# A residual that is transposed while its last projection still runs, into operand buffers of its own

## The reference

```python
x = x + merged @ w_out[l]                                    # block 1: "wo1";  block 2: "wo2"
h2 = rmsnorm(x, norm2_g[l])                                  # gain norm2_g;    block 2: g_mlp
x = x + jnp.square(jax.nn.relu(h2 @ w_mlp_in[l])) @ w_mlp_out[l]   # 2048 -> 8192 -> 2048: "h1","o1"; "h2","o2"
```

## Time and profile before

| | |
|---|---|
| median of 3 runs | 2964.06 us (2962.98 to 2964.64) |
| the profiled execution: time | 2963.64 us |
| the profiled execution: span, first to last instruction | 2961.7 us |
| PE busy | 2918.7 us, 99% of the span |
| PE weight loads | 2403.7 us, 81% |
| DVE, ACT busy | 1730.3 us (58%), 1367.7 us (46%) |
| mean granted clock of PE | 0.996 |
| DMA | 561 MB, mean 189 GB/s |

### The profile page before, as it was taken

One profiled execution on the slowest core, in us unless ns is written; L12 is line 12 of the kernel. 1 busy time (PEld: TensorE's weight loads), 2 busy tenths in 40 slices (PEclk: granted clock), 3 DMA queues, 4 the chain that ended last, 5 costly groups with the idle time before them and its releaser, 6 DMA issues.

```text
span 2961.7 us, 33940 instructions
## 1 busy us (share of the span) xinstructions
PE 2918.7 (99%) x13892; PEld 2403.7 (81%) x13892; DVE 1730.3 (58%) x1835; ACT 1367.7 (46%) x1570; POOL 60.3 (2%) x34
## 2 busy tenths in 40 slices
PE   8999999999999999999999999999999999999998
PEld 6788878888878888888888787888887888888886
DVE  6588854456655455554556678866655555455554
ACT  5544444554445444444445444444445444444443
POOL 1100000011000000000000000000000000000000
PEclk9999999999999999999999999999999999999999
DMA  8566755555655656555556656666555555656554
GB/s 281 165 195 196 203 167 184 179 160 188 209 174 185 198 174 203 185 181 188 195 179 228 182 170 192 198 192 210 179 201 180 190 185 183 197 175 203 186 179 155
DMA packets 290746, 561.01 MB, mean 189 GB/s; under 512 B 17696, under 2 KB 24608, under 8 KB 289952
## 3 DMA queue, kind: packets, MB, share of 16 engines
q1 hardware_dynamic: 290592, 558.85, 58.9%
HBM read 556.68 MB, written 2.10 MB: 189 GB/s over the span
## 4 chain that ended last, share of the span: by engine, by line
PE 77%; issue 18%; DVE 3%; POOL 1%; ACT 1%; DMA 0%; DVEq 0%; SPq 0%; ACTq 0%; POOLq 0%
PE ACC L569 75%; PE TB L525 2%; DVE WL L1232 1%; DVE CA L1667 1%; POOL QKV L1810 0%; ACT WH L820 0%; DMA RAW<-in_w_in_dram 0%; DVE X L1630 0%; DVE WGC L1715 0%; DVE X L1588 0%; PE TB L771 0%; ACT JK L838 0%; DMA SS<-in_x_t_dram 0%; POOL SS L1797 0%; POOL SS L1794 0%
## 5 line engine op out<-in xcount | busy, mean ns | idle before, releaser
L1232 DVE TENSOR_TENSOR WL<-RAW,WH 128x1024 fp32r<-128x1024 f32 (+1 forms) x1024 | 1252.7, 1239 | 883.1 <-ACT WH L820 881.5
L820 ACT ACTIVATE WH<-RAW 128x1024 fp32r<-128x1024 f32 (+1 forms) x1024 | 1063.3, 1054 | 973.3 <-PE ACC L569 913.5
L569 PE MATMUL ACC<-WH,XTH 128*128 128x512 f32 (+1 forms) x2720 | 1071.9, 394 | 30.3 <-DVE WL L1232 24.8
L569 PE MATMUL ACC<-WH,XTL 128*128 128x512 f32 (+1 forms) x2720 | 1060.1, 390 | 0.0
L569 PE MATMUL ACC<-WL,XTH 128*128 128x512 f32 (+1 forms) x2720 | 1058.7, 389 | 0.0
L569 PEld LDWEIGHTS ACC<-WH,XTH 128*128 128x128 f32 x2720 | 513.1, 189 | 139.5 <-DVE WL L1232 19.7
L569 PEld LDWEIGHTS ACC<-WH,XTL 128*128 128x128 f32 x2720 | 512.7, 189 | 107.4
L569 PEld LDWEIGHTS ACC<-WL,XTH 128*128 128x128 f32 x2720 | 513.5, 189 | 102.4
L569 PE MATMUL ACC<-WH,YAH 128*128 128x512 f32 x864 | 338.6, 392 | 0.0
L569 PE MATMUL ACC<-WH,YAL 128*128 128x512 f32 x864 | 336.5, 389 | 0.0
L569 PE MATMUL ACC<-WL,YAH 128*128 128x512 f32 x864 | 336.1, 389 | 0.0
(11 more groups left out here) (247 smaller groups left out, 1066.9 us busy)
## 6 DMA issues: line engine op xcount, KB each, us to landing
RAW<-in_w_in_dram SPq DMA_DIRECT2D x256, 512.0 KB, 4.3
RAW<-in_w_mlp_in_dram SPq DMA_DIRECT2D x128, 512.0 KB, 3.9
RAW<-in_w_mlp_out_dram SPq DMA_DIRECT2D x128, 512.0 KB, 4.5
RAW<-in_w_up_dram SPq DMA_DIRECT2D x128, 512.0 KB, 3.9
RAW<-in_w_down_dram SPq DMA_DIRECT2D x128, 512.0 KB, 4.6
RAW<-in_w_gate_dram SPq DMA_DIRECT2D x96, 512.0 KB, 4.0
RAW<-in_w_branch_dram SPq DMA_DIRECT2D x48, 512.0 KB, 4.4
RAW<-in_w_out_dram SPq DMA_DIRECT2D x32, 512.0 KB, 4.6
```

Source lines behind the costliest of these rows:

```text
L569: ins = e.matmul(ACC[:, 2 * (b % 2) + half, 0:n], p[:, k, xs], q[:, t, 0:n], start=(k == 0 and m == 0), stop=(k == nk - 1 and m == 2))
L820: e.activation(WH[u % NSPL][:, :, 0:n], RAW[u % NRAW][:, :, 0:n], ACT.Copy).then_inc(hi, 1)
L1232: e.tensor_tensor(l, r, h, ALU.subtract).then_inc(lo, 1)
```

## The change

Two buffer pairs are added, XBH1/XBL1 and XBH2/XBL2, [128, 16, 256] each. `turn` "x1" and "x3" write them, and all blocks of `h1` and `h2` multiply with them (`operands`). Laid out behind HB, they begin at bytes 165408 and 181792 (XBH1, XBL1) and 173600 and 189984 (XBH2, XBL2). The steps of "x1" and "x3" now stand behind units `last(w, c) + 2` and `+ 3` for each of the four blocks c, in the order that "x2" has: six of eight steps lie within `wo`, the last two behind the second and third unit of `h(0,0)`. `root` stays behind the last unit. In place of the wait for the last unit of `wo`, the first step waits for `mgv`, long past by then; "x2" waits for the last unit of `wo1`, also long past.

```diff
+    XB["1"] = sb("XBH1", [P, 16, L], F32R, m1), sb("XBL1", [P, 16, L], F32R, m1)
...
+    XB["2"] = sb("XBH2", [P, 16, L], F32R, m2), sb("XBL2", [P, 16, L], F32R, m2)
...
     for tag, w in (("x1", "wo1"), ("x3", "wo2")):
-        for _ in range(4):
-            at(("turn", tag), last(w, 3))
+        for c in range(4):
+            at(("turn", tag), last(w, c) + 2, 2)
         at(("root", tag), last(w, 3))
-        at(("turn", tag), last(w, 3) + 1, 4)
...
-            return XTH, XTL
+            return XB[kind[1]] if kind in ("h1", "h2") else (XTH, XTL)
...
-        def turn(task, done, gain):
+        def turn(task, ready, gain, to=XTH):
             for n in range(8):
                 if n == 0:
-                    multiplied(e, *done)
+                    ready()
...
-                        ins = e.activation(XTH[:, 2 * n + m, :], t[:, m * L:m * L + L], ACT.Copy, scale=gain[:, 2 * n + m:2 * n + m + 1])
+                        ins = e.activation(to[:, 2 * n + m, :], t[:, m * L:m * L + L], ACT.Copy, scale=gain[:, 2 * n + m:2 * n + m + 1])
...
-                 ("turn", "x1"): lambda: turn("x1", ("wo1", 3), VEC[:, V_N2:V_N2 + 16]),
-                 ("turn", "x2"): lambda: turn("x2", ("h1", 7, 1), gain_x2),
+                 ("turn", "x1"): lambda: turn("x1", lambda: e.wait_ge(mgv, 4), VEC[:, V_N2:V_N2 + 16], XB["1"][0]),
+                 ("turn", "x2"): lambda: turn("x2", lambda: multiplied(e, "wo1", 3), gain_x2),
...
-                 ("turn", "x3"): lambda: turn("x3", ("wo2", 3), VEC[:, V_MLP:V_MLP + 16]),
+                 ("turn", "x3"): lambda: turn("x3", lambda: e.wait_ge(mgv, 8), VEC[:, V_MLP:V_MLP + 16], XB["2"][0]),
```

More of the change, by code:

```diff
@@ L241, in build @@
     m1 = ExitStack()
-    YB, HB = {}, {}
+    YB, HB, XB = {}, {}, {}
     YB["1"] = sb("YBH1", [P, 8, L], F32R, m1), sb("YBL1", [P, 8, L], F32R, m1)
     HB["1"] = [sb(f"HB{i}1", [P, 2, 512], F32, m1) for i in range(2)]
+    XB["1"] = sb("XBH1", [P, 16, L], F32R, m1), sb("XBL1", [P, 16, L], F32R, m1)
     m1.close()
@@ L1034, in turn @@
                 if gain is None:
-                    e.activation(XTH[:, 2 * n:2 * n + 2, :], pair(t), ACT.Copy).then_inc(tx_hi, 1)
+                    e.activation(to[:, 2 * n:2 * n + 2, :], pair(t), ACT.Copy).then_inc(tx_hi, 1)
                 else:
                     for m in range(2):
-                        ins = e.activation(XTH[:, 2 * n + m, :], t[:, m * L:m * L + L], ACT.Copy, scale=gain[:, 2 * n + m:2 * n + m + 1])
+                        ins = e.activation(to[:, 2 * n + m, :], t[:, m * L:m * L + L], ACT.Copy, scale=gain[:, 2 * n + m:2 * n + m + 1])
                     ins.then_inc(tx_hi, 1)
@@ L1183, in _ @@
                  "gm0": lambda: gm_turn(0), "gm1": lambda: gm_turn(1), "at_t": at_turn, "yb": yb,
-                 ("turn", "m1"): lambda: turn("m1", ("gb", 3), None),
-                 ("turn", "x1"): lambda: turn("x1", ("wo1", 3), VEC[:, V_N2:V_N2 + 16]),
-                 ("turn", "x2"): lambda: turn("x2", ("h1", 7, 1), gain_x2),
-                 ("turn", "m2"): lambda: turn("m2", ("g2a", 3), None),
-                 ("turn", "x3"): lambda: turn("x3", ("wo2", 3), VEC[:, V_MLP:V_MLP + 16]),
+                 ("turn", "m1"): lambda: turn("m1", lambda: multiplied(e, "gb", 3), None),
+                 ("turn", "x1"): lambda: turn("x1", lambda: e.wait_ge(mgv, 4), VEC[:, V_N2:V_N2 + 16], XB["1"][0]),
+                 ("turn", "x2"): lambda: turn("x2", lambda: multiplied(e, "wo1", 3), gain_x2),
+                 ("turn", "m2"): lambda: turn("m2", lambda: multiplied(e, "g2a", 3), None),
+                 ("turn", "x3"): lambda: turn("x3", lambda: e.wait_ge(mgv, 8), VEC[:, V_MLP:V_MLP + 16], XB["2"][0]),
                  ("res", "wo1"): lambda: res_squares("wo1", R_1), ("res", "wo2"): lambda: res_squares("wo2", R_4),
@@ L1569, in branch_next, with turn @@
                 yield
-        def turn(task, gain):
+        def turn(task, gain, to=(XTH, XTL)):
             for n in range(8):
                 if gain is None:
-                    low_part(XTL[:, 2 * n:2 * n + 2, :], XTH[:, 2 * n:2 * n + 2, :], tx_hi, TX0[task] + n + 1, task, n)
+                    low_part(to[1][:, 2 * n:2 * n + 2, :], to[0][:, 2 * n:2 * n + 2, :], tx_hi, TX0[task] + n + 1, task, n)
                 else:
@@ L1579, in turn @@
                         k = 2 * n + m
-                        ins = e.scalar_tensor_tensor(out=XTL[:, k, :], in0=t[:, m * L:m * L + L], scalar=gain[:, k:k + 1],
-                                                     in1=XTH[:, k, :], op0=ALU.mult, op1=ALU.subtract)
+                        ins = e.scalar_tensor_tensor(out=to[1][:, k, :], in0=t[:, m * L:m * L + L], scalar=gain[:, k:k + 1],
+                                                     in1=to[0][:, k, :], op0=ALU.mult, op1=ALU.subtract)
                     freed(ins, task, n)
@@ L1739, in _ @@
                  ("branch", "b2a"): lambda: branch_next("b2a", "g2a", SG2, MG, 4),
-                 ("turn", "m1"): lambda: turn("m1", None), ("turn", "x1"): lambda: turn("x1", VEC[:, V_N2:V_N2 + 16]),
+                 ("turn", "m1"): lambda: turn("m1", None), ("turn", "x1"): lambda: turn("x1", VEC[:, V_N2:V_N2 + 16], XB["1"]),
                  ("turn", "x2"): lambda: turn("x2", gain_x2), ("turn", "m2"): lambda: turn("m2", None),
-                 ("turn", "x3"): lambda: turn("x3", VEC[:, V_MLP:V_MLP + 16]),
+                 ("turn", "x3"): lambda: turn("x3", VEC[:, V_MLP:V_MLP + 16], XB["2"]),
                  ("res", "wo1"): lambda: res_out("wo1"), ("res", "wo2"): lambda: res_out("wo2"),
```

## The result

The changed kernel takes 2976.16 us (median of 6 runs, 2974.72 to 2977.81), the kernel before 2964.35 us in the same rounds (2959.11 to 2965.51). The ratio is 1.0043, with a 95% interval of 1.003 to 1.0055: slower by 11.8 us. The forecast was 2977.2 us, range 2973 to 2982. The profiled execution took 2974.72 us, span 2972.7. Lines of `kernel.py` are one higher than before from the second added buffer on: line 569 is now 570, 1232 is 1233.

A forecast was written before the change was run, and what follows sets the result against it. PE, busy 99%, was taken as the bound, through its gaps and matmul pace. Terms -8.79 (stall and slow clock) + 1.4 (new wait) + 0.2 (places) + 20.3 (pace) = +13.1 us gave 2977.2 us, range 2973 to 2982.

The forecast's parts named there:

- The stall and its clock: From wo1 to h1 and wo2 to h2: PE's waits (5.73 us) and the slow clock behind them go, 8.79 us gained.
- the term of 3.06 us: Units behind PE's two 2.7 us gaps: matmuls at the lowered clock return to full pace, 3.06 us gained.
- The new wait: Third unit of h1 and h2: PE waits for a cut behind ACT's root and table load, 0.7 us each, 1.4 lost.
- Rival B: Crossings into h1 and h2: new wait longer or slow clock back, with XB's slow pace; 2980.4 us, chance 0.11.
- the wait of 2.23 us: A PE wait in the earlier trace followed by full-clock matmuls, cited for charging no slow clock to the new wait.
- The places: Within wo: four more places, twice, where a step interrupts PE's matmuls, 0.03 us each, 0.2 us lost.
- The pace: h1 and h2: 3072 matmuls load from XB at YB's pace instead of XT's, 6.6 ns each, 20.3 us lost.
- Rival A: h1 and h2: XB reads at XT's pace, so the pace term is 0; -7.1 us, 2957.0 us, chance 0.11.
- C: h1 and h2: XB slow only in part, about 10 us lost, 2967 us, no difference; chance 0.04.
- a multiple of 64: Loaded buffers: YB and XB begin 32 bytes past one, offered as one possible reason for the 6.6 ns slower pace.
- the upper part of the partition: Loaded buffers: YB and XB lie above byte 131200, offered as the other possible reason for the 6.6 ns slower pace.

The follow-up runs named there:

- e4: The changed kernel's buffers with the step and root order of the kernel before: 2981.64 us, 1.0058 of the kernel before.
- e9: The kernel before with 96 unused bytes ahead of ST, so YB begins at a multiple of 128: 2955.76 us, ratio 0.9973.
- e5: The changed kernel with 96 unused bytes ahead of ST, so XB and YB begin at multiples of 128: 2948.2 us, 0.9949 of the kernel before.
- e2: The kernel before with 32 unused bytes ahead of ST: 2960.66 us, ratio 0.9987.
- e3: The kernel before with XT moved by 32 bytes and all behind it by 64: 3009.35 us, ratio 1.0153.
- e8: e5 with the root of x1 and x3 four units later: 2949.01 us, 0.995 of the kernel before.
- e10: e5 with the moving operands WH and WL alone moved by 32 bytes: 3020.39 us in one execution.
- e6: e5 with all buffers from X on moved by 32 bytes, all distances kept: 2949.62 us, 0.9951 of the kernel before.
- e11: e5 with loaded pairs at chosen distances past the moving operand (YB1 128, XB1 64, YB2 32, XB2 256 bytes): 2966.3 us in one execution.
- e12: e5 with loaded pairs at chosen distances past the moving operand (YB1 384, XB1 16, YB2 96, XB2 192 bytes): 2966.62 us in one execution.
- e7: e5 with loaded pairs offset from a multiple of 128 (YB1 4, XB1 16, XB2 64, YB2 96 bytes; low parts another 128): 2966.89 us, one execution.

## Why the prediction was right

**The stall and its clock, 8.79 us.** Both waits of 2.7 us and both slow stretches are gone. Taken alone, the order gave 5.7 us (e4 against the changed kernel) and 8.3 us (e9 against e5) for a forecast of 8.79 - 1.4 - 0.2 = 7.2. Each is the difference of two ratios whose intervals are some 3 to 4.5 us to either side, so 5.7 and 8.3 can't be told apart. The traces say more. From PE's wait near 630 us to the one near 1590, and from the one near 1815 us to the end, e5 is 3.4 and 3.2 us shorter than e9, 6.6 in all; the changed kernel is 1.9 and 3.3 shorter than e4. The 1.9 belongs to the crossing of e4 at which the clock stayed full. For the slow clock after the gap is not certain: in the five kernels of this study that keep the 2.7 us wait (before, e2, e3, e4, e9) the low clock followed it in 8 of 10 places, so the term of 3.06 us is what one trace showed and not what every execution pays.

**The new wait, 0.7 us each.** It stands where the working put it, and is 0.60 and 0.61 us long; it brought no slow clock back. Rival B is out. e8 shows that it comes from the root ahead of the cut. That no slow clock followed waits this short held in all traces; the wait of 2.23 us that the prediction named beside them was luck of that trace, as the last section shows.

**The places, 0.2 us.** Steps lie within `wo1` as planned, with 19.08 us for 84 matmuls and no wait between them.

**The pace, 20.3 us.** The size was right: 6.6 to 6.75 ns for each of 3072 matmuls in the trace, 17.5 us in the time of e4, whose trace lacks one slow stretch (some 1.6 us). Rival A is out, and so is C: XB's pace is 233.3 ns in every block. The reason offered was not: of the two that the prediction left open, a multiple of 64 and the upper part of the partition, the upper part is refuted by e5, where XB lies there at 226.9 ns (and not needed, by e3 and e10), and the multiple of 64 by e6, where every buffer is 32 off and fast. The term held because XB lies at the same distance from WH and WL as YB does: the rest by 256 is 32 for all of YB and XB and 128 for WH and WL, 160 apart. The number, read from YB, was no luck; that XB came to lie at YB's distance was, for the reason as it was given: a change that put XB elsewhere than YB modulo 256 would have been priced wrongly. In e11's second layer both lie in the upper part; XB2, at a distance of 256, takes 226.8 ns and YB2, at 32, 233.3. One side figure of the prediction does not follow from its own numbers: with the pace term at 2.9 us rival A would be 4.2 us faster, less than its bound of 5.9; the limit lies at 1.2 us, 0.4 ns a matmul, not 0.9.

**The whole.** By one trace of each, from the kernel before to the changed one: +0.9 us up to 630 us, before anything is changed; +6.1 over the first layer's crossing and MLP; -2.2 between the layers; +6.2 from there to the end. The two layers give 12.3 us, the forecast had 13.1. The -2.2 is none of the change's order or pace: at 1754 us the kernel before has a wait of 1.92 us and a slow stretch behind it (windows: clock 0.70), the changed kernel a wait of 1.36 us there at full clock.

## What to carry to other kernels

Before a product is moved to another buffer, look in the trace for two stages that differ in the buffer alone and divide: here a pace term of 3% on 3072 of the 13892 matmuls cost 20.3 us and outweighed the 8.8 us of stall and slow clock. Where PE is the bound with fp32r operands of these shapes, give the loaded tiles and the moving ones the same rest by 256 bytes; here it cost 96 unused bytes in a partition, turned 0.4% slower into 0.5% faster than before (2948.2 us), and gave the kernel before 0.27%. When work is spread into the stage ahead, list what stays behind its last unit: here the root and its table load, which can go later; that took both waits away, though no time was measured to go with them.

## What the runs showed that was not expected

- The pace of back-to-back fp32r matmuls (128x128 loaded, 512 columns moving) depends on the distance between the loaded and the moving operand within 256 bytes: 226.8 ns at 0, 228.9 at 192, 232.4 to 234.2 at 32, 64, 96, 128, 160 and 224. The profile shows 188 ns for a weight load at both paces. The Trainium skill (SBUF — State Buffer, "Who interferes with whom") gives PE two independent read ports, one for the moving operand and one for weight loads; in e10 moving one operand by 32 bytes slowed all matmuls, so here the measurement decides. Why the two disturb each other was not tried: no run separates a conflict of PE's two reads from something in the load itself.
- At a distance of 16 (e12) the pace has two values, 226.7 and 233.3 ns, and keeps one for many matmuls before it changes; e7's XB1, at 16 and 144, does the like. What makes it change stays open.
- The clock fell behind some waits of PE and not behind others of the same length. Over the 14 traces of this study, after the first 100 us: behind waits of 2.7 us in 8 of 10 places, behind 2.08 to 2.25 us in 18 of 28, behind 1.3 to 1.94 us in 1 of 13 (the 1.92 us before; 1.94 us in e11 did not), and behind none of the shorter ones. The wait of 2.23 us of the earlier trace rows, at full clock there, is one of the 28. The same wait in the kernel before, then in e5:

```profile
1651.50:1656.00 4.50, 4.49 (x22) 3.73 (x23) 2.23 (x2) 1.00 (x2) 0.00 (x0) 1.00 0.77 226
```

```profile
1645.40:1650.00 4.60, 4.57 (x14) 3.62 (x15) 2.24 (x2) 0.00 (x0) 0.00 (x0) 0.63 0.71 231
```

A single trace is thus no ground for calling a wait of this length free of the slow clock.
